# A two-layer decoder trunk with a product-key expert mixer: the table of gates built in device memory by GpSimd's accumulating transfers instead of by one-hot products on TensorE

## The chip, the cores and the metric

The kernel runs on one core of one Trainium2 chip. The metric is the device time of one execution in microseconds (us), the median of several runs. Five engines run side by side: TensorE (PE in the profile, with its weight loads apart as PEld), VectorE (DVE), ScalarE (ACT), GpSimd (POOL) and SyncE (SP), which here only issues transfers. Sixteen DMA engines move the data.

## The reference, cut to what matters

Two layers, 256 tokens, 1024 channels, all in float32. Each layer has a small token mixer (a gated convolution, then a pooling mixer) and then the part that takes most of the time, a retrieval over 16384 experts:

```python
def peer_ffn(h, w_q, k1, k2, u_tab, v_tab):        # T = 256 tokens, 8 heads, top 16, 128 keys a side
    q = (ht @ w_q).reshape(T, PEER_HEADS, 2, D_HALF)
    s1 = jnp.einsum('thd,nd->thn', q[:, :, 0], k1)
    s2 = jnp.einsum('thd,nd->thn', q[:, :, 1], k2)
    v1, i1 = lax.top_k(s1, PEER_TOPK)
    v2, i2 = lax.top_k(s2, PEER_TOPK)
    cand = (v1[..., :, None] + v2[..., None, :]).reshape(T, PEER_HEADS, PEER_TOPK * PEER_TOPK)
    sc, flat = lax.top_k(cand, PEER_TOPK)
    e1 = jnp.take_along_axis(i1, flat // PEER_TOPK, axis=-1)
    e2 = jnp.take_along_axis(i2, flat % PEER_TOPK, axis=-1)
    idx = e1 * N_KEYS + e2
    gate = jax.nn.softmax(sc.astype(jnp.float32), axis=-1)
    ...
    act = jax.nn.gelu(jnp.einsum('td,thkd->thk', xc, u_tab[ic]), approximate=False)
    out = jnp.einsum('thk,thkd->td', gc * act, v_tab[ic])
```

## The kernel before

Nothing is gathered: since 256 tokens times 128 picks touch most experts, each layer multiplies every token with all 16384 rows of `u_tab` and of `v_tab`, 128 rows to a tile. A layer runs through stages: the mixer's products, 16 "query" tiles, 128 "up" tiles, 128 "down" tiles. Every up tile gives a 128 x 256 block of expert activations (128 experts by 256 tokens), which ACT passes through Gelu into the buffer `acts`. The activations are then multiplied by a table of gates (softmax weight of expert e for token t, zero nearly everywhere), and the down tiles multiply the result with the 128 rows of `v_tab`.

Each weight tile (512 KB) takes the same road. SP loads it into one of four slots of `raw` (`load`, which waits on `low_ready` for the slot to be free); ACT rounds it to fp32r in `high` (`ahead`, `round_tile`); DVE computes the rest `low = raw - high` (`slot`, `rest_of`); PE makes three products for one (high x high, low x high, high x low). ACT and DVE work three tiles ahead (`AHEAD`). An up tile is 24 products of 256 columns, a down tile 12 of 512 columns. The order of all work is written out by hand, engine by engine, and engines meet at semaphores that count.

The picks are found on DVE beside the first 76 up tiles (`retrieval`): one pass of its loop per pair of score rows, with a `beside()` (one more tile's `low`) between the steps, nine to a pass; `numbers` turns a pass's picks into expert numbers a pass later. A softmax over all picks is made once at the end: ACT's Exp waits for `soft_in` before up tile 74, with a load of the Exp table and another of the Gelu table. Then PE transposes numbers and gates (L1289), and the table of gates is built in PSUM (`gp`) as a product of one-hot matrices: for 8 tokens at a time (a set) DVE compares the numbers with an iota (`hots`: `hot1` holds three bf16 parts of the gate at the row of e1, `hot2` a one at that of e2), PE multiplies them (`scatter`, L1267, 24 products of 64 columns a set), and DVE multiplies the activations by the result (`weigh`, L893). Half the table is built beside up tiles 80 to 127, two sets after every third tile; the other half beside the first 64 down tiles, two sets after every fourth. The last 64 down tiles of layer 0 share their time with the next layer's modulation sums (w_mod loads and L591 on DVE).

GpSimd clears a few constants at the start and is idle for the rest.

Of the kernel before, what the change touches and what calls it, by code (L numbers as in the profile page):

```python
# [5 lines left out]
F32 = mybir.dt.float32  # L6
# [7 lines left out]
P = 128  # L14
# [17 lines left out]
SETS = HALF // 2  # L32
SET = T // SETS
PAIRS = SET // 2
TURN = 76
FIRST_SET = 80
PARTS = 3
# [48 lines left out]
def program(nc, small, x_in, k_t, w_mod, conv_in, conv_out, query, up, down, pool_in, pool_group, pool_out,  # L86
# [8 lines left out]
    with ExitStack() as ctx:  # L95
# [22 lines left out]
        idx1 = sb("idx1", [P, T], BF16)  # L118
        idx2 = sb("idx2", [P, T], BF16)
        gate = sb("gate", [P, T // 2, PARTS, 2], BF16)  # L120
        hot1 = sb("hot1", [P, 2, PAIRS, PARTS, HALF, 2], BF16)
        hot2 = sb("hot2", [P, 2, PAIRS, P, 2], BF16)


        gate_rest = hot2[:].rearrange("p a b c d -> p (a b c d)").bitcast(F32)[:, 0:T]
# [44 lines left out]
        GT = part(o + 1600, T)  # L170
        SUM = part(o + 1856, ROWS)
        RS = part(o + 1872, ROWS)
        twice = hot2[:, 0, 0]
# [41 lines left out]
        pick_done, turned, turned_out = sem("pick_done"), sem("turned"), sem("turned_out")  # L215
        hot1_ready = sem("hot1_ready")
        scattered, weighted = sem("scattered"), sem("weighted")
# [26 lines left out]
        def _(sp):  # L244
# [55 lines left out]

            for layer in range(LAYERS):
# [15 lines left out]
                run(layer, "up", KEYS)  # L317
# [38 lines left out]
        @block.gpsimd  # L356
        def _(pool):
            nc.gpsimd.memset(ones[:], 1.0).then_inc(const_ready, 1)
            nc.gpsimd.memset(eps[:], EPS).then_inc(const_ready, 1)
            nc.gpsimd.memset(zeros[:], 0.0).then_inc(const_ready, 1)  # L360
            nc.gpsimd.memset(macc[:, 2:MODS].rearrange("p m n -> p (m n)"), 0.0).then_inc(const_ready, 1)

        @block.scalar
        def _(act):
# [88 lines left out]
            for layer in range(LAYERS):  # L453
# [44 lines left out]
                gelus(8, (TURN - RING - 8) // RING)  # L498
                for s in range(RING):
                    if s == 2:  # L500
                        act.wait_ge(soft_in, layer + 1)
                        nc.scalar.activation(SC, SC, ACT.Exp).then_inc(soft_exp, 1)
                        load_table(ACT.Gelu)
                    gelu(0, TURN - RING, s)


                gelus(TURN, 2 * HEADS // RING)
                act.wait_ge(turned, layer + 1)
                gelus(TURN + 2 * HEADS, (KEYS - TURN - 2 * HEADS) // RING)
# [8 lines left out]
                for half in range(2):  # L518
                    first = half * HALF

                    act.wait_ge(weighted, (2 * layer + half + 1) * SETS)
                    for s in range(AHEAD):
                        act.wait_ge(product, n0 + first + s + 1 + (RING - 1 - s if half == 0 else 0))
                        weight(first + s, s)
                    with act.Fori(0, HALF // RING - 1) as i:
                        for s in range(RING):
                            ahead(i, n0 + first, s)
                            weight(i * RING + (first + s + AHEAD), (s + AHEAD) % RING)
                    last = n0 + first + HALF - RING
                    if half == 1:  # L530
                        load_table(ACT.Sqrt)
                    ahead(0, last, 0)
                    weight(first + HALF - 1, RING - 1)
                    if half == 0:
                        for s in range(1, RING):
                            ahead(0, last, s)
# [24 lines left out]
        def _(dve):  # L561
# [20 lines left out]
            link(nc.vector.tensor_tensor(cact[:], ctmp[:], sm[:, C_C:C_C + DC], ALU.mult))  # L582
            link(nc.vector.tensor_copy(twice, sm[:, C_IOTA:C_IOTA + KEYS].unsqueeze(2).broadcast_to([P, KEYS, 2])))
# [855 lines left out]
```

## Time and profile before

| | |
|---|---|
| median of 3 runs | 1902.19 us (1902.03 to 1902.82) |
| the profiled execution, its own time | 1903.38 us |
| span of its trace | 1901.6 us |
| PE busy | 1860.2 us, 98% of the span |
| DVE busy | 1524.4 us, 80% |
| ACT busy | 858.2 us, 45% |
| POOL busy | 4.0 us |
| moved by the DMA engines | 370.46 MB, 195 GB/s on average |

The table is one execution, taken by the hardware profiler. A share of busy time is an average over all stages; the rows further down are taken stage by stage. Up tiles run in this trace from about 200 to 600 us in layer 0 and from about 1112 to 1512 us in layer 1, down tiles from 601 to 963 us and from 1514 to 1876 us.

### The profile page before, as it was taken

How to read it: one execution, taken by the hardware profiler on the slowest of the kernel's cores; microseconds unless marked ns; L12 is line 12 of the kernel's file. 1: busy time of each engine (PE TensorE's matmuls, PEld its weight loads, DVE VectorE, ACT ScalarE, POOL GpSimd, SP SyncE). 2: the span in 40 equal slices, each digit the busy share in tenths (PEclk: the TensorE clock that was granted, in tenths of full speed). 3: DMA queues.
4: the chain of work that ended last, by engine and by line, in shares of the span. 5: the costliest groups of instructions: out<-in, count | busy, mean ns of one | idle time of the engine just before them, and what ended most of it. 6: DMA issues, size and time to landing. Idle time of an engine off the chain costs nothing.

```text
span 1901.6 us, 39850 instructions
## 1 busy us (share of the span) xinstructions
PE 1860.2 (98%) x14863; PEld 1726.2 (91%) x14863; DVE 1524.4 (80%) x2634; ACT 858.2 (45%) x1281; POOL 4.0 (0%) x8
## 2 busy tenths in 40 slices
PE   5999999999999999999999999999999999999998
PEld 5999999999999888888889999999999988888887
DVE  7986689888888888888868768889788888885555
ACT  3335444454434444455444544444434444445453
POOL 0000000000000000000000000000000000000000
PEclk9999999999999999999988999999999999999999
DMA  7976455555444555688834745555544455555552
GB/s 301 335 277 236 154 179 185 177 176 170 153 166 139 171 176 167 235 325 319 321 127 168 262 158 177 179 185 185 168 146 165 138 172 165 176 187 190 197 189 99
DMA packets 101344, 370.46 MB, mean 195 GB/s; under 512 B 11168, under 2 KB 11552, under 8 KB 100640
## 3 DMA queue, kind: packets, MB, share of 16 engines
q1 hardware_dynamic: 100848, 367.43, 55.5%
q10 hardware_dynamic: 432, 2.23, 0.3%
q8 instruction: 34, 0.56, 0.1%
q14 instruction: 30, 0.25, 0.0%
HBM read 366.47 MB, written 3.15 MB: 194 GB/s over the span
## 4 chain that ended last, share of the span: by engine, by line
PE 91%; DVE 5%; DMA 2%; issue 1%; ACT 1%; SPq 0%; DVEq 0%; ACTq 0%
PE ps L1156 46%; PE acc L1315 36%; PE gp L1267 5%; DVE acts L591 2%; DVE low L572 2%; PE ps L1135 1%; PE gp L1077 1%; DMA raw<-conv_in 1%; PE gp L1256 1%; DMA acts<-w_mod 1%; PE gp L1099 0%; ACT high L371 0%; DMA raw<-conv_out 0%; PE acc L1094 0%; DVE acts L952 0%
## 5 line engine op out<-in xcount | busy, mean ns | idle before, releaser
L572 DVE TENSOR_TENSOR low<-raw,high 128x1024 fp32r<-128x1024 f32 x596 | 727.7, 1222 | 320.6 <-ACT high L371 318.5
L371 ACT ACTIVATE high<-raw 128x1024 fp32r<-128x1024 f32 x593 | 626.7, 1057 | 483.0 <-PE acc L1315 383.3
L1156 PE MATMUL ps<-mov_h,high 128*128 128x256 f32 x2656 | 761.2, 287 | 9.9 <-DVE mov_l L680 5.4
L1156 PE MATMUL ps<-mov_l,high 128*128 128x256 f32 x2656 | 755.4, 284 | 0.0
L1156 PE MATMUL ps<-mov_h,low 128*128 128x256 f32 x2656 | 755.2, 284 | 0.0
L1156 PEld LDWEIGHTS ps<-mov_h,high 128*128 128x128 f32 x2656 | 513.4, 193 | 11.5 <-issue 8.2
L1156 PEld LDWEIGHTS ps<-mov_l,high 128*128 128x128 f32 x2656 | 513.7, 193 | 0.0
L1156 PEld LDWEIGHTS ps<-mov_h,low 128*128 128x128 f32 x2656 | 513.6, 193 | 0.0
L1315 PE MATMUL acc<-high,mov_h 128*128 128x512 f32 x1024 | 402.6, 393 | 1.0 <-DVE mov_l L1009 0.8
L1315 PE MATMUL acc<-high,mov_l 128*128 128x512 f32 x1024 | 399.0, 390 | 0.0
L1315 PE MATMUL acc<-low,mov_h 128*128 128x512 f32 x1024 | 398.6, 389 | 0.0
L483 ACT ACTIVATE acts<-ps 128x256 f32 (+1 forms) x256 | 98.5, 385 | 432.2 <-PE ps L1156 432.2
L1315 PEld LDWEIGHTS acc<-high,mov_h 128*128 128x128 f32 x1024 | 192.2, 188 | 41.1 <-DVE mov_l L1009 2.2
L1315 PEld LDWEIGHTS acc<-high,mov_l 128*128 128x128 f32 x1024 | 192.2, 188 | 40.6
L1315 PEld LDWEIGHTS acc<-low,mov_h 128*128 128x128 f32 x1024 | 192.4, 188 | 38.9
L881 DVE TENSOR_TENSOR hot<-hot,gate 128x1536 bf16<-128x1536 bf16 x128 | 121.9, 952 | 0.0
L591 DVE SCALAR_TENSOR_TENSOR acts<-acts,cact 128x1024 f32<-128x1024 f32 x86 | 110.1, 1280 | 5.1 <-DMA acts<-w_mod 4.7
L1009 DVE TENSOR_TENSOR mov_l<-acts,mov_h 128x256 fp32r<-128x256 f32 x256 | 106.5, 419 | 2.7 <-ACT mov_h L515 2.7
L1267 PEld LDWEIGHTS gp<-hot 128*128 128x128 bf16 x3072 | 96.4, 97 | 9.7 <-issue 8.4
L1267 PE MATMUL gp<-hot 128*128 128x64 bf16 x3072 | 104.1, 193 | 0.0
L515 ACT ACTIVATE mov_h<-acts 128x256 fp32r (+1 forms) x256 | 101.5, 399 | 0.0
L877 DVE TENSOR_TENSOR hot<-sm,idx 128x1024 bf16<-128x1024 bf16 x128 | 87.7, 685 | 0.0
(116 smaller groups left out, 802.4 us busy)
## 6 DMA issues: line engine op xcount, KB each, us to landing
raw<-up SPq DMA_DIRECT2D x256, 512.0 KB, 3.2
raw<-down SPq DMA_DIRECT2D x256, 512.0 KB, 4.0
acts<-w_mod SPq DMA_DIRECT2D x84, 512.0 KB, 5.8
raw<-query SPq DMA_DIRECT2D x32, 512.0 KB, 3.9
raw<-conv_in SPq DMA_DIRECT2D x24, 512.0 KB, 6.8
acts<-w_mod SPq DMA_DIRECT2D x6, 1024.0 KB, 14.7
raw<-conv_out SPq DMA_DIRECT2D x8, 512.0 KB, 7.0
raw<-pool_in SPq DMA_DIRECT2D x8, 512.0 KB, 3.9
```

The costliest lines, as they stand in the source:

```text
L371: nc.scalar.activation(flat(high[s]), tile_row(s), ACT.Copy).then_inc(high_ready, 1)
L483: nc.scalar.activation(A[:, bass.ds(i * (RING * T) + (first + s) * T, T)], ps[:, s % 2, 0:T], ACT.Gelu).then_inc(evac_act, 1)
L515: nc.scalar.activation(mov_h[:, s], A[:, bass.ds(g * T, T)] if not isinstance(g, int) else A[:, g * T:(g + 1) * T], ACT.Copy).then_inc(wh_ ...
L572: nc.vector.tensor_tensor(flat(low[n % RING]), tile_row(n % RING), flat(high[n % RING]).bitcast(F32), ALU.subtract).then_inc(low_ready, 1)
L591: return nc.vector.scalar_tensor_tensor(macc[:, m], tile, c, macc[:, m], ALU.mult, ALU.add)
L877: nc.vector.tensor_tensor(hot2[:, u], number(0, P), over(idx2, P), ALU.is_equal)
L881: nc.vector.tensor_tensor(hot1[:, u].rearrange("p h n e two -> p (h n) e two"), eq.unsqueeze(2).broadcast_to([P, PAIRS, PARTS, HALF, 2]).r ...
L1009: nc.vector.tensor_tensor(mov_l[:, s], A[:, g * T:(g + 1) * T], mov_h[:, s].bitcast(F32), ALU.subtract).then_inc(wl_ready, 1)
L1077: ins = nc.tensor.matmul(gp[:, 1, m * DC + c:m * DC + c + 1], macc[:, m, c * P:(c + 1) * P], ones[:, 0:1], start=True, stop=True)
L1156: ins = nc.tensor.matmul(dst, w[s][:, c], m[:, mv], start=(first and n == 0), stop=(last and n == 2), skip_group_check=skip)
L1267: ins = nc.tensor.matmul(gp[:, u, j * HALF:(j + 1) * HALF], hot2[:, u, j // 2, :, j % 2], hot1[:, u, j // 2, n, :, j % 2], start=(n == 0), ...
L1315: ins = nc.tensor.matmul(acc[:, b, :], w[:, s, tok], flat(v[s])[:, cols], start=False, stop=(closing and n == 2), skip_group_check=True)
```

## The change

The table of gates is no longer a product on PE. It lies in device memory, one table of 16.8 MB a layer, [128 partitions e2] x [128 e1] x [256 tokens] in float32.

SP clears it with 32 transfers of 512 KB a layer from a buffer of zeros: those of layer 0 behind every second query tile (8) and each of the first 24 up tiles, those of layer 1 behind every second one of the next 64 up tiles of layer 0. The retrieval is put in order of heads: a pass of its loop now covers both halves of the tokens for one head, has its own softmax (an Exp on ACT before up tiles 11, 20, ... 74, each with its two table loads), and ends with the addresses in `dest` and the gates in `gates`. For each head GpSimd issues 32 indirect transfers (2 halves of the tokens x 16 picks), each of which adds 128 single floats, one from each partition, to the table at 128 addresses; before a half's 16 transfers it waits for all of the same half's earlier ones to have landed. When all 256 of a layer have landed, GpSimd fetches the table back in 64 pieces of 256 KB (two tiles of experts each) through a ring of four buffers `wt`, and DVE multiplies the activations by each piece (`weigh`, one piece beside each of the first 62 down tiles). The one-hot products, the transposes and the sets are gone.

```diff
+            def clear(layer, at):
+                cols = bass.ds(at, CHUNK) if not isinstance(at, int) else slice(at, at + CHUNK)
+                sp.dma_start(rows[layer][:, cols].rearrange("p (r n) -> p r n", n=2 * T),
+                             nothing[:].unsqueeze(1).broadcast_to([P, CHUNK // (2 * T), 2 * T])).then_inc(zeroed[layer], 16)
...
+                if layer == 0:
+                    for j in range(24):
+                        load(0, "up", j, j % RING)
+                        clear(0, (8 + j) * CHUNK)
+                    with sp.Fori(0, CHUNKS // 2) as i:
+                        for s in range(RING):
+                            load(0, "up", i * RING + (24 + s), s)
+                            if s % 2:
+                                clear(1, i * (2 * CHUNK) + s // 2 * CHUNK)
...
+            def add_gates(layer, p, tc):
+                if layer or p:
+                    pool.wait_ge(landed[tc], 16 * TOPK * (layer * HEADS + p))
+                for k in range(TOPK):
+                    col = (TC * p + tc) * TOPK + k
+                    nc.gpsimd.indirect_dma_start(
+                        table[layer], bass.IndirectOffsetOnAxis(ap=DEST[:, col:col + 1], axis=0),
+                        GT[:, col:col + 1], None, compute_op=ALU.add).then_inc(landed[tc], 16)
+            def fetch(layer, i, s, free):
+                if free is not None:
+                    pool.wait_ge(weighted, free)
+                at = i * (WRING * 2 * T) + s * 2 * T
+                cols = bass.ds(at, 2 * T) if not isinstance(at, int) else slice(at, at + 2 * T)
+                nc.gpsimd.dma_start(wt[:, s], rows[layer][:, cols]).then_inc(wt_in[s], 16)
+            for layer in range(LAYERS):
+                pool.wait_ge(zeroed[layer], 16 * CHUNKS)
+                for p in range(HEADS):
+                    pool.wait_ge(picked, layer * HEADS + p + 1)
+                    for tc in range(TC):
+                        add_gates(layer, p, tc)
+                for tc in range(TC):
+                    pool.wait_ge(landed[tc], 16 * TOPK * HEADS * (layer + 1))
+                for s in range(WRING):
+                    fetch(layer, 0, s, layer * WPAIRS - WRING + s + 1 if layer else None)
...
-                gelus(8, (TURN - RING - 8) // RING)
-                for s in range(RING):
-                    if s == 2:
-                        act.wait_ge(soft_in, layer + 1)
-                        nc.scalar.activation(SC, SC, ACT.Exp).then_inc(soft_exp, 1)
+                exps = {(HEADS + 1) * p + 11: p for p in range(HEADS)}
+                for j in range(8, SCRATCH):
+                    if j in exps:
+                        p = exps[j]
+                        act.wait_ge(soft_in, HEADS * layer + p + 1)
+                        sc = SC[:, TC * p * TOPK:TC * (p + 1) * TOPK]
+                        nc.scalar.activation(sc, sc, ACT.Exp).then_inc(soft_exp, 1)
                         load_table(ACT.Gelu)
...
+            def weigh(layer, j):
+                dve.wait_ge(wt_in[j % WRING], 16 * (layer * (WPAIRS // WRING) + j // WRING + 1))
+                a = A[:, 2 * j * T:2 * (j + 1) * T]
+                nc.vector.tensor_tensor(a, a, wt[:, j % WRING], ALU.mult).then_inc(weighted, 1)
...
                 dve.wait_ge(evac_act, 2 + layer * (16 + KEYS) + 16 + HALF)
-                k = 0
-                for j in range(FIRST_SET, KEYS):
-                    slot(n0 + j)
-                    if (j - FIRST_SET) % 3 == 2:
-                        two_sets(0, k)
-                        k += 2
+                weigh(layer, 0)
+                weigh(layer, 1)
...
                 for j in range(HALF):
                     slot(n0 + j)
-                    if j + AHEAD < HALF:
-                        low_weight(j + AHEAD)
-                    if j % 4 == 2:
-                        two_sets(1, j // 4 * 2)
+                    if j + 2 < WPAIRS:
+                        weigh(layer, j + 2)
+                    low_weight(j + AHEAD)
...
-                        up_tile(i, FIRST_SET, s, 12)
-                        if s % 3 == 1:
-                            scatter(0, i, s // 3 * 2, 8)
-                            scatter(0, i, s // 3 * 2 + 1, 8)
```

On PE, at the end of the second tile of four in the first half of the down stage, these rows stand before (L1315 are a down tile's products, L1267 those of two sets, 24 each; the others are loop registers):

```order
1451 L1315 MATMUL acc<-low,mov_h 128x512
1452 L1315 MATMUL acc<-high,mov_l 128x512
1453 L1264 ISA
1454 L1267 MATMUL gp<-hot 128x64 x24
1455 L1264 REGISTER_ALU
1456 L1267 MATMUL gp<-hot 128x64 x24
1457 L1322 REGISTER_ALU
1458 L1323 REGISTER_ALU
1459 L1315 MATMUL acc<-high,mov_h 128x512
```

and now (L1299 are a down tile's products):

```order
913 L1299 MATMUL acc<-low,mov_h 128x512
914 L1299 MATMUL acc<-high,mov_l 128x512
915 L1306 REGISTER_ALU
916 L1307 REGISTER_ALU
917 L1299 MATMUL acc<-high,mov_h 128x512
```

One tile's products now follow the last one's with nothing between; the same holds at the up tiles from 80 on.

On DVE, in the retrieval's second pass, behind the last search for candidates (L827 before) and at the next tile's `low` (L572), these rows stand before:

```order
211 L821 MAX acts<-acts 128x8 x2
212 L769 TENSOR_REDUCE acts<-acts 128x2x32
213 L572 TENSOR_TENSOR low<-raw,high 128x1024
214 L827 MAX_INDEX acts<-acts 128x8 x2
215 L572 TENSOR_TENSOR low<-raw,high 128x1024 x2
```

and now (L906 is that search, L627 that `low`; `gates` and `dest` are what GpSimd's transfers read):

```order
218 L900 MAX acts<-acts 128x8 x2
219 L831 RECIPROCAL acts<-acts 128x2
220 L833 TENSOR_REDUCE acts<-acts 128x2x32
221 L627 TENSOR_TENSOR low<-raw,high 128x1024
222 L906 MAX_INDEX acts<-acts 128x8 x2
223 L911 TENSOR_TENSOR acts<-acts 128x32
224 L840 SCALAR_TENSOR_TENSOR acts<-acts 128x32
225 L842 TENSOR_TENSOR gates<-acts 128x32
226 L846 SCALAR_TENSOR_TENSOR dest<-acts,tok 128x32
227 L627 TENSOR_TENSOR low<-raw,high 128x1024 x2
```

A pass has gained short instructions of its own softmax and addresses (five of them here, two more earlier in the pass), and the first head's addresses are there only at the end of the second pass.

On POOL, before, the last instructions are the clearing of constants:

```order
8 L360 MEMSET zeros 128x128
9 L361 MEMSET acts 128x4096
10 L95 UNCONDITIONAL_BRANCH
```

and now, for layer 0 (with what the instruction waits for; the rows of heads 1 to 6 read like those of head 7, which are the last three ahead of the fetches):

```order
10 L387 MEMSET nothing 128x512
11 L396 DMA table<-gates,dest 4194304x1 [waits picked,zeroed0]
12 L396 DMA table<-gates,dest 4194304x1 x31
13 L396 DMA table<-gates,dest 4194304x1 [waits landed0,picked]
...
38 L396 DMA table<-gates,dest 4194304x1 x15
39 L396 DMA table<-gates,dest 4194304x1 [waits landed1]
40 L396 DMA table<-gates,dest 4194304x1 x15
41 L406 DMA wt<-table 128x512 [waits landed1,landed0]
42 L406 DMA wt<-table 128x512 x3
```

POOL's queue now holds 256 indirect transfers a layer, and no fetch can leave before the last of them has landed.

## Rows read from the trace of the kernel before

**Rows 1.** The page: busy time, and the chain that ended last, by line.

```profile
PE 1860.2 (98%) x14863; PEld 1726.2 (91%) x14863; DVE 1524.4 (80%) x2634; ACT 858.2 (45%) x1281; POOL 4.0 (0%) x8
...
PE ps L1156 46%; PE acc L1315 36%; PE gp L1267 5%; DVE acts L591 2%; DVE low L572 2%; PE ps L1135 1%; PE gp L1077 1%; DMA raw<-conv_in 1%; PE gp L1256 1%; DMA acts<-w_mod 1%; PE gp L1099 0%; ACT high L371 0%; DMA raw<-conv_out 0%; PE acc L1094 0%; DVE acts L952 0%
```

**Rows 2.** The chain in order of time: start us, length us, what.

```profile
229.19 201.59 PE ps L1156 x1680
430.78 0.66 PE gp L1289 x6
444.40 8.71 PE ps L1156 x72
454.58 8.71 PE ps L1156 x72
608.51 11.01 PE acc L1315 x48
621.00 11.01 PE acc L1315 x48
801.37 160.77 PE acc L1315 x708
1141.75 201.59 PE ps L1156 x1680
```

**Rows 3.** The same chain where the up stage ends and the down stage begins.

```profile
597.04 2.96 PE ps L1156 x24
...
601.31 5.74 PE acc L1315 x24
```

**Rows 4.** Stretches: length, busy time (x) of PE, PEld, DVE, ACT, POOL, PEclk, DMA share, GB/s.

```profile
229.00:430.00 201.00, 201.00 (x1677) 201.00 (x1676) 174.48 (x467) 98.31 (x144) 0.00 (x0) 1.00 0.51 180
608.00:793.00 185.00, 185.00 (x1405) 153.84 (x1402) 162.20 (x241) 80.78 (x119) 0.00 (x0) 1.00 0.52 170
802.00:962.00 160.00, 160.00 (x708) 132.47 (x707) 132.30 (x155) 79.97 (x118) 0.00 (x0) 1.00 0.87 320
```

**Rows 5.** DVE's groups, 225 to 400 us: shapes, count, busy us, mean ns, idle before.

```profile
L572 DVE TENSOR_TENSOR low<-raw,high 128x1024 fp32r<-128x1024 f32 x60 | 73.1, 1218 | 22.9 <-ACT high L371 22.9
L754 DVE TENSOR_TENSOR acts<-acts,sm 128x1024 f32<-128x1024 uint32 x7 | 8.5, 1208 | 0.0
```

**Rows 6.** Groups over the whole run.

```profile
L1009 DVE TENSOR_TENSOR mov_l<-acts,mov_h 128x256 fp32r<-128x256 f32 x256 | 106.5, 419 | 2.7 <-ACT mov_h L515 2.7
L893 DVE TENSOR_TENSOR acts<-acts,gp 128x512 f32<-128x512 f32 x128 | 81.8, 681 | 0.0
```

**Rows 7.** DVE in order of time: the second pass's end, and a short instruction.

```profile
255.70 0.42 DVE L827 FIND_INDEX8 acts<-acts 128x8 uint32<-128x256 f32 x1
256.61 1.23 DVE L572 TENSOR_TENSOR low<-raw,high 128x1024 fp32r<-128x1024 f32 x1 [0.48 <-ACT high L371]
413.33 0.17 DVE L749 TENSOR_SCALAR acts<-acts 128x32 uint32<-128x32 uint32 x1
```

**Rows 8.** ACT in order of time around the Exp of layer 0.

```profile
419.70 1.28 ACT L502 ACT_TABLE_LOAD   x1
421.43 1.28 ACT L386 ACT_TABLE_LOAD   x1
423.92 0.37 ACT L483 ACTIVATE acts<-ps 128x256 f32<-128x256 f32 x1
```

**Rows 9.** One issue on SP's queue (start, length), then transfers' median us to landing.

```profile
850.44 0.33 SPq L256 DMA_DIRECT2D raw<-down  x1
...
out<-acts SPq DMA_DIRECT2D x4, 256.0 KB, 2.1
acts<-k_t ACTq DMA_DIRECT2D x1, 128.0 KB, 3.1
```

**Rows 10.** DMA, first 12 us: GB/s by slice, then queues (packets, MB, share).

```profile
GB/s 0 0 0 0 0 0 71 81 104 355 438 413 409 355 314 328 396 423 410 410 451 396 300 382 437 437 437 410 369 396 355 396 423 410 355 437 410 410 437 410
q10 hardware_dynamic: 144, 0.13, 5.7%
```

More of the change, by code:

```diff
@@ L117, in program @@
         zeros = sb("zeros", [P, P], BF16)
[L118 to L125, printed above, removed]
+        GT = sb("gates", [P, T], F32)
+        DEST = sb("dest", [P, T], U32)
+        tok = sb("tok", [P, TC], F32)
+        wt = sb("wt", [P, WRING, 2 * T], F32)
+        nothing = sb("nothing", [P, 2 * T], F32)
+        table = [nc.dram_tensor(f"table{n}", (P * KEYS * T, 1), F32, kind="Internal").ap() for n in range(LAYERS)]
+        rows = [v.rearrange("(p n) one -> p (n one)", p=P) for v in table]
         iota = sm[:, C_IOTA:C_IOTA + KEYS].bitcast(BF16).rearrange("p (n two) -> p n two", two=2)
@@ L214, in program @@
         soft_in, soft_exp = sem("soft_in"), sem("soft_exp")
[L215 to L217 removed]
+        picked, pick_done = sem("picked"), sem("pick_done")
+        zeroed = [sem(f"zeroed{n}") for n in range(LAYERS)]
+        landed = [sem(f"landed{n}") for n in range(TC)]
+        wt_in = [sem(f"wt_in{n}") for n in range(WRING)]
+        weighted = sem("weighted")
         wh_ready, wl_ready = sem("wh_ready"), sem("wl_ready")
@@ L361, in _ @@
             nc.gpsimd.memset(macc[:, 2:MODS].rearrange("p m n -> p (m n)"), 0.0).then_inc(const_ready, 1)
+            nc.gpsimd.memset(nothing[:], 0.0).then_inc(const_ready, 1)
+            def add_gates(layer, p, tc):
[22 more added lines that the diff above has]
+                    fetch(layer, 0, s, layer * WPAIRS - WRING + s + 1 if layer else None)
+                with pool.Fori(0, WPAIRS // WRING - 1) as i:
+                    for s in range(WRING):
+                        fetch(layer, i + 1, s, i * WRING + (layer * WPAIRS + s + 1))
         @block.scalar
@@ L516, in weight @@
                                          else A[:, g * T:(g + 1) * T], ACT.Copy).then_inc(wh_ready, 1)
[L518 to L536, printed above, removed]
+                for s in range(AHEAD):
+                    act.wait_ge(product, n0 + RING)
+                    act.wait_ge(weighted, layer * WPAIRS + s // 2 + 1)
+                    weight(s, s)
+                with act.Fori(0, KEYS // RING - 1) as i:
+                    for s in range(RING):
+                        ahead(i, n0, s)
+                        act.wait_ge(weighted, i * (RING // 2) + (layer * WPAIRS + (s + AHEAD) // 2 + 1))
+                        weight(i * RING + (s + AHEAD), (s + AHEAD) % RING)
+                last = n0 + KEYS - RING
+                load_table(ACT.Sqrt)
+                ahead(0, last, 0)
+                weight(KEYS - 1, RING - 1)
                 def evac(b):
@@ new lines, in down_banks @@
+                def down_banks(s, banks, closing):
+                    for b in banks:
+                        tok = slice(b % 2 * P, (b % 2 + 1) * P)
+                        cols = slice(b // 2 * 512, (b // 2 + 1) * 512)
+                        for n, (v, w) in enumerate(((high, mov_h), (low, mov_h), (high, mov_l))):
+                            ins = nc.tensor.matmul(acc[:, b, :], w[:, s, tok], flat(v[s])[:, cols], start=False,
+                                                   stop=(closing and n == 2), skip_group_check=True)
+                        if closing and b < 3:
+                            ins.then_inc(acc_done, 1)
+                    return ins
```

238 lines of the change are left out of this document (86 added, 152 removed).

## The prediction

> **What bounds the kernel now.** I read the page first. PE is busy for 98% of the span, and the chain that ended last is PE for nine tenths: 46% up tiles (L1156), 36% down tiles (L1315), 5% one-hot products (L1267) [rows 1]. So the share that the change removes lies on the path itself. Then I read the chain in order of time for prices without overlap. The steady up stage is one piece, 1680 products in 201.59 us: 0.120 us each, 2.880 us a tile. The steady down stage is 708 products in 160.77 us: 0.2271 us each, 2.725 us a tile [rows 2]. The stretches show what the other engines have left there: DVE is busy 87% beside the retrieval, 88% in the first half of the down stage, 83% in the second; the DMA engines 51%, 52% and 87% [rows 4].
>
> **What is removed.** In the up stage three tiles with two sets take 454.58 - 444.40 = 10.18 us, three plain tiles 8.64: two sets cost 1.54 us, 16 times a layer, 24.6 us. In the down stage four tiles with two sets take 621.00 - 608.51 = 12.49 us, four plain ones 10.90: 1.59 us, 16 times, 25.4 us. The transposes are 0.66 us [rows 2]. Per layer 50.7 us, together 101.4 us, all of it on PE's path.
>
> **What is added on PE: nothing.** The rest counts only where something becomes late.
>
> DVE, retrieval. A pass gains seven short instructions. The nearest row, 32 elements, is 0.17 us [rows 7]; with waits for their predecessors between them I take up to 0.25, so 1.2 to 1.75 us a pass. DVE's idle time there is 22.9 us in 60 tiles, 3.4 us per pass of nine tiles, and all of it is waiting for ACT's `high` [rows 5]. That covers it: nothing. Without the cover, each further us a pass costs 16 us in all.
>
> ACT, softmax. Exp and two table loads hold ACT from 419.70 to 422.71 and the Gelu of tile 74 ends at 423.92 + 0.37 = 424.29 [rows 8]. Tile 76 needs it at 229.19 + 68 x 2.880 = 425.03 [rows 2], and the 201.59 us piece ran through that place without a gap. This now happens eight times a layer, never more often than every nine tiles: nothing, with 0.74 us to spare. `soft_in` leaves DVE before the `low` of that tile's successor, so ACT finds it there.
>
> DVE, down stage. A tile needs low 1.22, mov_l 0.42 and the product with a fetched piece; the nearest row is L893, 128x512, 0.68 [rows 5, 6]. 2.32 us against 2.725: nothing.
>
> Clears. In the query stage and beside the first 24 up tiles 1.049 MB have to move per 2.88 us, 364 GB/s. With reads alone the engines gave 355 to 451 in most slices after the start [rows 10], and 320 at a share of 0.87, which would be 368 at full share [rows 4]. Writes of this kind aren't in the trace. Between nothing and, at 320 GB/s, 40 tiles x 0.40 = 16 us; I take 3, since the demand meets the full-share rate and a load has four slots to land in. SP's queue gains one issue of 0.33 us per tile [rows 9]: nothing. The fetches bring the down stage to 192 + 96 = 288 GB/s, less than the 320 beside which PE ran without a gap: nothing.
>
> **The queue that decides: POOL.** It issues 256 indirect transfers a layer, and the first down tile stands behind the last. When can it begin? The first head's addresses follow the second pass's last search, which ends at 256.12, by about 1 us: 257 [rows 7]. The last clear of layer 0 goes out at about the same time and takes some 4 us more: 261. Layer 1 is the same, 912.56 us later [rows 2], without the clear. When must it end? Tile 8 starts at 229.19, so up tiles now end at 229.19 + 120 x 2.880 = 574.8; before, the first down product came 1.31 us behind the last up tile [rows 3], so 576.1. Ahead of it stand: landing 2.1 and the fetch 2.1 (the quickest kind in the trace), its issue 0.33 [rows 9], the product 0.68, mov_h and mov_l 0.9: about 6.1, so the last transfer must leave by 570. That is 309 us in layer 0 and 313 in layer 1, **1.21 us per transfer**. Each 0.1 us more costs 256 x 2 x 0.1 = 51 us, and the gain is gone at 1.21 + 98/512 = 1.41 us. Heads come every nine tiles (25.9 us), so below 0.81 us POOL waits for DVE and it doesn't matter.
>
> The trace has no transfer from POOL, so its pitch has to be bounded. From below the nearest row is an issue on SP's hardware queue, 0.33 us; from above a transfer waited out each time, 3.1 us for 128 KB from issue to landing [rows 9]. POOL writes 128 descriptors by program and reads 128 addresses, but doesn't wait for landings within a head (16 transfers to a semaphore, two semaphores by turns). I take about 1 us, the geometric middle of the two ends. Then 256 us fit into 309, and the cost is nothing.
>
> The Trainium skill, DMA: Bandwidth & Descriptors, Latency and other measured facts, gives about 1 us to the first byte from GpSimd; were that the pitch, the queue would be hidden, with 0.2 us a transfer to spare. The same page, Anatomy of one DMA, fits about 2.0 us fixed per transfer; were they not overlapped, it would be 512 x 0.79 = 404 us of stall. No row of this case tells which.
>
> **The sum.** 1903.4 (the profiled execution's own time, 1.2 above the median of the runs) - 101.4 + 3 = **1805 us**.
>
> **Rivals.**
>
> *POOL's own pitch is over 1.41 us: slower.* One mechanism: at the end of each up stage PE stands until the last head has landed. For it: software descriptors, two sides, one address read for every float. Against it: three issues of SP would fit into the allowance. At 1.8 us: 1805 + 512 x 0.59 = 2107; at 2.07: 2245.
>
> *POOL is late by less than it gains (1.21 to 1.41):* 1810 to 1900.
>
> *DVE holds POOL off.* Of the 175 us of the retrieval's stretch L572 and L754, which read two operands from SBUF for 1.2 us each, take 81.6, 47% [rows 5]. Should POOL's read of addresses have to wait for such an instruction's end, that is 0.47 x 0.6 = 0.28 us per transfer, and POOL's own pitch may only be 0.93. With an own pitch of 1.2 it would give 1805 + 512 x 0.27 = 1943, slower. The trace can't show it, since POOL is idle. The Trainium skill, SBUF — State Buffer, Who interferes with whom, says just this of DVE instructions with two SBUF inputs beside a GpSimd instruction that reads SBUF; it infers that descriptor writing isn't touched.
>
> *The DMA engines can't take the small adds.* The 144 packets of the ACT queue in the first 12 us, 0.9 KB each, took 5.7% of 16 engines: 76 ns each [rows 10]. 128 adds are 128 reads and 128 writes, 16 packets an engine, 1.2 us per transfer. 256 of them and the weight stream's 51% [rows 4] need 312 + 176 = 488 us of 346: 142 us late a layer, 1805 + 284 = 2089. Against it: packets in flight overlap, so 76 ns may be mostly waiting.
>
> **How the numbers follow.** I know POOL's pitch only between 0.33 and 3.1 us, so I spread it evenly over the ratio: 58% lies below 1.21, 65% below 1.41, 82% below 2.07. The lock would put the first two at 46% and 55% or so, and the engines' load takes some more. So: hidden 0.46; late but less than the gain 0.08; within 0.2% (about what a measurement of this kernel can tell from no change) 0.02; own pitch over 1.41 0.29; lock 0.07; engines 0.08. Faster 0.54, same 0.02, slower 0.44. The range goes from 1797 (no cost for the clears, and 5 us for gaps at the stages' joints that may shrink) to 2245, beyond which 0.18 remain. Cases of both signs hold much; the hidden case's own range is 1797 to 1825.
>
> **What the new profile would show.** L1267 gone from the chain, and 120 up tiles from the ninth on as one piece of 346 us (right); a gap of PE between the last up product and the first down product of more than 2 us, with POOL behind it (wrong: then the distance from one indirect transfer to the next beside it is the pitch, and which of the three it is shows in the DMA share and in whether it is shorter where DVE runs no two-operand work). DVE's idle time in the retrieval still behind `high`; if PE waits for `low` there, a pass has become too long. PE waiting for `high` behind DMA in the first 24 up tiles would be the clears.

## The result, and the profile after

The changed kernel takes 2233.87 us (median of four executions, 2233.14 to 2235.66) against 1902.49 us before: a ratio of 1.174 (95% interval 1.172 to 1.176). I had predicted 1805. The time lies in the stated range, on the side of the rivals: not faster by 5%, but slower by 17%.

The page of the changed kernel, busy time and the costliest group of POOL, answers to [rows 1]:

```profile
PE 1760.5 (79%) x11779; PEld 1635.3 (73%) x11779; DVE 1305.8 (58%) x2341; ACT 895.7 (40%) x1337; POOL 960.8 (43%) x649
...
PEclk9999999999655589999999999999985557999999
...
L396 POOL DMA_INDIRECT table<-gates,dest x512 | 887.2, 1733 | 801.9 <-DVE dest L846 385.3
```

PE's work shrank from 1860.2 to 1760.5 us, as it should. But its share of the span fell from 98% to 79%, and in two places its clock line drops to 5: there PE does nothing. The waits name the place (engine, line, what was waited for: us in all, times, longest):

```profile
PE acc L1299 <- DVE mov_l L1028: 432.0, 2, 218.7
DVE acts L929 <- DMA wt<-table: 430.6, 3, 217.5
```

Twice, once a layer, the first down product waits 213 to 219 us for its moving operand `mov_l`, which waits for the first fetched piece of the table. The longest wait of DVE has almost the same length, so nothing lies between but the chain that the prediction had listed. What the fetch waited for stands in POOL's order of time (start, length, instruction, idle time before it), layer 0, first the beginning and then the end of the table:

```profile
265.90 1.78 POOL L396 DMA_INDIRECT table<-gates,dest  x1 [260.74 <-DMA table<-nothing]
267.98 1.56 POOL L396 DMA_INDIRECT table<-gates,dest  x1 [0.30 <-issue]
...
785.80 1.55 POOL L396 DMA_INDIRECT table<-gates,dest  x1 [0.30 <-issue]
789.41 2.25 POOL L406 DMA_DIRECT2D wt<-table  x4 [2.06 <-DMA table<-gates,dest]
```

The 256 transfers of layer 0 begin at 265.90 and end at 787.35, 521 us, where 309 were free. And stretches (length, busy time and count of PE, PEld, DVE, ACT, POOL, clock, DMA share, GB/s) show where they were when PE ran out of up tiles, with [rows 4] as their counterpart:

```profile
229.00:575.00 346.00, 346.00 (x2887) 345.96 (x2886) 240.24 (x567) 184.94 (x273) 265.71 (x142) 1.00 0.86 247
576.00:788.00 212.00, 0.00 (x0) 0.00 (x0) 0.00 (x0) 0.00 (x0) 176.63 (x115) 0.51 0.22 3
```

Up to 575 us PE works without a gap; POOL has got through 142 of 256. Then only POOL works, 115 transfers in 212 us (one counts on both sides), 1.85 us each: 1.55 busy and 0.30 of "issue" before the next. So the reader can see the whole of the excess in one row: four engines at zero.

### The profile page after: what moved, and what is told of

Same layout as the page of the kernel before. It is cut to its first block and busy times, and to the rows that moved or that the text cites. A ratio compares the mean times of both kernels' runs of the same rounds, so it can differ in the third digit from the quotient of the medians.

```text
span 2233.7 us, 34220 instructions
## 1 busy us (share of the span) xinstructions
PE 1760.5 (79%) x11779; PEld 1635.3 (73%) x11779; DVE 1305.8 (58%) x2341; ACT 895.7 (40%) x1337; POOL 960.8 (43%) x649
## 5 line engine op out<-in xcount | busy, mean ns | idle before, releaser
L396 POOL DMA_INDIRECT table<-gates,dest x512 | 887.2, 1733 | 801.9 <-DVE dest L846 385.3
L627 DVE TENSOR_TENSOR low<-raw,high 128x1024 fp32r<-128x1024 f32 x596 | 727.5, 1223 | 444.4 <-ACT high L430 443.7
L1299 PE MATMUL acc<-high,mov_h 128*128 128x512 f32 x1024 | 400.5, 391 | 432.0 <-DVE mov_l L1028 432.0
L1299 PEld LDWEIGHTS acc<-high,mov_h 128*128 128x128 f32 x1024 | 193.1, 189 | 472.2 <-DVE mov_l L1028 432.3
L1299 PE MATMUL acc<-low,mov_h 128*128 128x512 f32 x1024 | 399.8, 390 | 0.0
L1299 PE MATMUL acc<-high,mov_l 128*128 128x512 f32 x1024 | 399.6, 390 | 0.0
L929 DVE TENSOR_TENSOR acts<-acts,wt 128x512 f32<-128x512 f32 x128 | 87.5, 684 | 430.6 <-DMA wt<-table 430.6
L542 ACT ACTIVATE acts<-ps 128x256 f32<-128x256 f32 (+1 forms) x256 | 98.1, 383 | 343.5 <-PE ps L1170 343.3
L1299 PEld LDWEIGHTS acc<-high,mov_l 128*128 128x128 f32 x1024 | 193.0, 189 | 40.7
L1299 PEld LDWEIGHTS acc<-low,mov_h 128*128 128x128 f32 x1024 | 193.1, 189 | 39.9
L406 POOL DMA_DIRECT2D wt<-table x128 | 69.1, 541 | 267.5 <-DVE acts L929 263.1
L1091 PEld LDWEIGHTS gp<-ones,acts 128*128 128x128 f32 x192 | 25.7, 215 | 11.3 <-DVEq L658 9.8
```

Source lines behind the costliest of these rows:

```text
L396: nc.gpsimd.indirect_dma_start(table[layer], bass.IndirectOffsetOnAxis(ap=DEST[:, col:col + 1], axis=0), GT[:, col:col + 1], None, compute ...
L406: nc.gpsimd.dma_start(wt[:, s], rows[layer][:, cols]).then_inc(wt_in[s], 16)
L542: nc.scalar.activation(A[:, bass.ds(i * (RING * T) + (first + s) * T, T)], ps[:, s % 2, 0:T], ACT.Gelu).then_inc(evac_act, 1)
L627: nc.vector.tensor_tensor(flat(low[n % RING]), tile_row(n % RING), flat(high[n % RING]).bitcast(F32), ALU.subtract).then_inc(low_ready, 1)
L929: nc.vector.tensor_tensor(a, a, wt[:, j % WRING], ALU.mult).then_inc(weighted, 1)
L1091: ins = nc.tensor.matmul(gp[:, 1, m * DC + c:m * DC + c + 1], macc[:, m, c * P:(c + 1) * P], ones[:, 0:1], start=True, stop=True)
```

## The experiments

Each series ran the kernel before beside it: 1900.73 us beside e1, e3, e4 and e5, 1901.80 beside e2, e6 and e7, 1901.62 beside e8 and e9. So times of different series compare to about 2 us. e3, e4, e5, e7 and e8 are one execution each.

**e1: 8 of the 16 picks of each head** (128 transfers a layer; the gates of the other picks are left out).

```diff
+PICKS = 8
...
-                for k in range(TOPK):
+                for k in range(PICKS):
```

> The changed kernel with only the first 8 of each head's 16 picks added to the table (128 transfers a layer instead of 256; the other half of the gates is left out). Theory Q, the queue's length: POOL leaves about one transfer per 2.04 us from 266 us on, so the last leaves at about 266 + 261 = 527 us, before the up stage ends at 575; both waits of PE for the first down tile vanish and the time is 1805 us (1798 to 1812). Rival R, something else that the change adds costs too (clears, eight Exps a layer, a busier DVE, the fetches): the two waits vanish but the time stays clearly above, 1820 to 1900. Rival D, the transfers' landing and the DMA engines and not POOL's issuing set the end: the wait shrinks by less than the 128 transfers' 238 us a layer would allow, and a wait of tens of us stays.

1800.61 us (four executions, 1798.36 to 1802.58), ratio 0.947 (0.945 to 0.948). In the chain in order of time (start, length) the joint has closed up: 119 up tiles are one piece, and 123 down tiles the next:

```profile
231.09 342.73 PE ps L1171 x2856
578.14 334.86 PE acc L1300 x1476
```

With the queue hidden, the kernel is where the prediction's sum puts it. Rival D, the landing of the transfers, is out too: PE waits 1.1 us in both layers together. So the removal is worth what was read from [rows 2], and clears, fetches, the longer passes and the eight Exps cost nothing that can be seen. What failed is POOL's queue alone.

**e2: 12 of 16 picks** (192 a layer, the rest left out), the same edit with 12.

> Only 12 of the 16 picks of each head are added to the table (192 transfers a layer instead of 256; the gates of the last four picks are left out of the computation). Theory F (the whole excess is the POOL queue: 1.55 us a transfer and 0.30 between two, longer while VectorE is busy): about 144 of the 192 are out when the up products end at 575 us, the other 48 take 1.85 us each, 89 us, and then the fetch and the first weighting, some 8 us; so the down products start some 97 us late in each layer, less what the changed kernel's own start needs there, and the kernel takes 1805 + 2 x 96, about 1997 us. Rival C (the cost of the table is not the number of transfers before the deadline, but sets in with the last ones, for instance because the additions to one place queue up): the time lies in proportion between that of 8 picks, 1801, and that of 16, 2234, which gives 2017, or stays near 2234.

1998.38 us (two executions), ratio 1.051 (1.049 to 1.053). The expectation by theory F was 1997; PE waits 99.7 us a time at most:

```profile
PE acc L1300 <- DVE mov_l L1029: 195.9, 2, 99.7
```

The time isn't in proportion to the transfers: 128 cost nothing, the next 64 a layer 198 us in all, the next 64 another 235. It is a queue with a deadline, some 140 transfers long. Rival C's proportion would have given 2017.

**e3: the same transfers as plain writes** (a gate that two heads share is kept once instead of summed).

```diff
-                        GT[:, col:col + 1], None, compute_op=ALU.add).then_inc(landed[tc], 16)
+                        GT[:, col:col + 1], None).then_inc(landed[tc], 16)
```

> The same 256 transfers a layer, but plain writes instead of additions (a gate that two heads share is kept once only). Theory Q: POOL's own time is that of writing 128 pairs of descriptors and reading 128 addresses, the addition is done by the DMA engines: 1.55 us busy and 1.85 us from one to the next, as before, time 2234 us within 10. Rival A, the addition costs POOL descriptors of its own (a second read of each cell): 1.2 us busy or less, and 512 x 0.35 = 180 us or more off the time, 2055 us.

**e4: 64 rows a transfer** (the gates of half of the tokens are left out).

```diff
-                        GT[:, col:col + 1], None, compute_op=ALU.add).then_inc(landed[tc], 16)
+                        GT[0:64, col:col + 1], None, compute_op=ALU.add).then_inc(landed[tc], 16)
```

> Each of the 256 transfers a layer takes the picks of 64 tokens only, partitions 0 to 63 (the gates of the other half of the tokens are left out). Theory row: POOL's 1.55 us are mostly per row: 0.8 us busy, 1.1 from one to the next, 256 of them (282 us) fit and the time is 1805 us (within 10). Rival fixed: most of the 1.55 us is paid per instruction: 1.3 us busy or more, pitch 1.6 or more, and a wait of PE of at least 100 us a layer stays, 2010 us or more.

e3 took 1942.76 us and e4 2131.33: in both the rival held and not the theory. POOL's instructions on the table (ns, least, median, most; first and last start), of the changed kernel, of e3 and of e4:

```profile
L396 POOL DMA_INDIRECT table<-gates,dest x512: 1537/1547/3237, 265.9 to 1861.2; - x171
```

```profile
L396 POOL DMA_INDIRECT table<-gates,dest x512: 954/959/3344, 264.2 to 1568.9; - x171
```

```profile
L396 POOL DMA_INDIRECT table<-gates,dest x512: 1391/1407/3347, 264.1 to 1756.5; - x171
```

The addition costs POOL itself 0.59 of its 1.55 us a transfer. Half the rows save only 0.14: by these two points, an estimate, about 2.2 ns a row stand on a fixed 1.27 us ((1547 - 1407) / 64, and 1547 less 128 of these). And even plain writes, 0.96 + 0.30 = 1.26 us apart at best, miss the allowance of 1.21; PE still waited 140.6 us in e3, which is 2% slower than the kernel before.

**e5: does DVE hold POOL off?** Extra DVE work in the stall, results unused: in layer 0 additions that take `nothing` twice, in layer 1 sums over `nothing`.

```diff
+                if layer == 0:
+                    for q in range(150):
+                        last = did(nc.vector.tensor_tensor(spare[:, q % 2 * 512:(q % 2 + 1) * 512], nothing[:], nothing[:],
+                                                           ALU.add))
...
+                else:
+                    for q in range(150):
+                        last = did(nc.vector.tensor_reduce(single[:, q % 2:q % 2 + 1], nothing[:], AX_X, ALU.add))
...
```

> The changed kernel, whole, with 150 short DVE instructions of 512 elements put into the stretch in which every other engine waits for POOL: in layer 0 additions of two operands from SBUF (0.68 us each, about 102 us), in layer 1 reductions of one operand (about 98 us). Theory L, a transfer that starts while DVE reads two operands from SBUF waits for that instruction's end: in layer 0's stretch the mean of a transfer rises from 1.55 us to 1.8 or 1.9, the wait of PE there grows by about 15 us, and in layer 1's stretch it stays at 1.55 us. Rival: any DVE work slows POOL: both rise. Rival: none does, and the longer transfers of the up stage come from the weight stream in the DMA engines: both stay at 1.55 us and the time at 2234 us.

2234.88 us, and POOL's transfers seemed to keep their length beside both kinds (mean 1572 and 1571 ns). That spoke against the rival of the lock. The means hide a difference, though: 1571 takes in one transfer of 2.56 us that had begun beside the last `low`, and beside the sums themselves all are 1.54 to 1.56. Beside the additions three are longer, the first one (1.86 us at 576.44) and these two:

```profile
645.20 1.56 POOL L397 DMA_INDIRECT table<-gates,dest  x1 [0.30 <-issue]
647.07 2.09 POOL L397 DMA_INDIRECT table<-gates,dest  x1 [0.30 <-issue]
649.47 2.09 POOL L397 DMA_INDIRECT table<-gates,dest  x1 [0.30 <-issue]
651.87 1.54 POOL L397 DMA_INDIRECT table<-gates,dest  x1 [0.30 <-issue]
```

The trace of the changed kernel itself spoke for the lock more plainly. DVE and POOL in order of time in the up stage of layer 0:

```profile
504.57 1.23 DVE L627 TENSOR_TENSOR low<-raw,high 128x1024 fp32r<-128x1024 f32 x1 [1.65 <-ACT high L430]
507.68 1.23 DVE L627 TENSOR_TENSOR low<-raw,high 128x1024 fp32r<-128x1024 f32 x1 [1.88 <-ACT high L430]
```

```profile
504.64 2.58 POOL L396 DMA_INDIRECT table<-gates,dest  x1 [0.30 <-issue]
507.52 1.55 POOL L396 DMA_INDIRECT table<-gates,dest  x1 [0.30 <-issue]
```

The first transfer begins 0.07 us into L627 and lasts 1.03 us longer than 1.55; the second is 0.16 us ahead of the next L627 and lasts 1.55. Where two-operand instructions stand one behind the other, the hold can reach over more than one: the transfer at 271.70 begins with an L627 and is held over it and over the 512 elements of L876 behind it.

```profile
271.70 1.22 DVE L627 TENSOR_TENSOR low<-raw,high 128x1024 fp32r<-128x1024 f32 x1
272.84 0.68 DVE L876 TENSOR_TENSOR acts<-acts 128x512 f32<-128x512 f32 x1
```

```profile
271.70 3.24 POOL L396 DMA_INDIRECT table<-gates,dest  x1 [0.30 <-issue]
```

So I looked for what the probe had been missing.

**e7: two different operands, and larger ones.**

```diff
+                def two(n, q, in1):
+                    return did(nc.vector.tensor_tensor(spare[:, q * n:(q + 1) * n], A[:, 0:n], in1, ALU.add))
+
+                if layer == 0:
+                    for q in range(80):
+                        last = two(512, q % 2, nothing[:])
...
+                    for q in range(40):
...
+                        last = two(1024, 0, A[:, 1024:2048])
+                        for h in range(2):
+                            last = did(nc.vector.tensor_reduce(single[:, h:h + 1], nothing[:], AX_X, ALU.add))
+                else:
+                    for q in range(60):
...
+                        last = two(1024, 0, A[:, 1024:2048])
+                    for q in range(80):
...
+                        last = two(512, q % 2, A[:, 0:512])
```

> The changed kernel, with VectorE given extra work while it waits for the table (results unused). Layer 0: 80 additions of 512 elements of two different buffers (acts and nothing), end to end, then 40 times one addition of 1024 elements of two places of acts and two sums over 512 elements of one operand. Layer 1: 60 additions of 1024 elements end to end, then 80 additions of 512 elements that take the same place of acts twice. Theory L2 (a transfer that is issued while a VectorE instruction with two different operands runs is held until that ends; the same operand twice doesn't do it): the transfers beside the first three kinds last longer, by some 0.3 us on the average beside 512 elements and 0.6 beside 1024, in the mixed part only those that begin during the addition, and those beside the last kind stay at 1.55. Rival S (size: only instructions of 1024 elements hold it): the first kind leaves 1.55, the 1024 ones lengthen it. Rival G (what holds the transfers in the up stage is not VectorE's operands but the output buffer, which PE or the DMA engines share there): all stay at 1.55 to 1.57, as with the earlier probe. The kernel's time rises by what the additions cost the queue, by 0 (rival G) to about 50 us.

2276.63 us, 43 more than without the additions. POOL beside the 512-element additions, and beside the 1024-element ones with sums between:

```profile
596.81 1.55 POOL L397 DMA_INDIRECT table<-gates,dest  x1 [0.30 <-issue]
598.66 1.54 POOL L397 DMA_INDIRECT table<-gates,dest  x1 [0.30 <-issue]
...
700.53 2.14 POOL L397 DMA_INDIRECT table<-gates,dest  x1 [0.30 <-issue]
702.98 2.15 POOL L397 DMA_INDIRECT table<-gates,dest  x1 [0.30 <-issue]
```

By the letter this was rival S, the size, and two different buffers don't matter. But DVE's own rows show a trap:

```profile
595.61 10.53 DVE L1024 TENSOR_TENSOR mov_l<-acts,nothing 128x512 fp32r<-128x512 f32 x17
```

17 additions in 10.53 us are 0.619 each, and three of them 1.858: just the distance of two transfers. In step with them, every transfer begins at a joint between two additions and has nothing to wait for. e5's additions had the same pitch (28 in 17.29 us). Once in step, such a train looks the same with a lock and without; only the transfers that fall out of step tell, as the two in e5 did. In layer 1 of e7, too, the second transfer beside the additions of 512 elements that take one place twice is held, and then they fall into step:

```profile
1755.14 2.09 POOL L397 DMA_INDIRECT table<-gates,dest  x1 [0.30 <-issue]
1757.54 1.56 POOL L397 DMA_INDIRECT table<-gates,dest  x1 [0.30 <-issue]
```

**e8: pitches that don't divide 1.85**, one place of `acts` taken twice: 1024 elements in layer 0, 736 in layer 1, 64 additions and then 64 sums.

```diff
+                for kind, n in (((two, 1024), (total_of, 1024)), ((two, 736), (total_of, 736)))[layer]:
+                    for q in range(64):
+                        last = kind(n)
...
```

> The changed kernel with extra VectorE work in the stall (results unused), one after the other: layer 0 has 64 additions of 1024 elements that take one and the same place of acts twice, then 64 sums over 1024 elements of one operand; layer 1 the same with 736 elements. In both earlier probes three instructions of 512 elements took 1.856 us (0.619 each), and a transfer with its gap takes 1.85: the transfers could begin at a boundary every time without being held, so these two probes could not show a hold. 1024 elements (about 1.22 us) and 736 (about 0.88) don't divide 1.85 so. Theory L3 (a transfer is held until the end of any VectorE instruction of two operands in whose course it is issued, whatever its size and operands; one operand doesn't do it): beside the additions the transfers follow each other at a multiple of the additions' pitch, about 2.44 us for 1024 elements and 2.6 for 736, and last longer by what is missing, 0.6 and 0.7 us; beside the sums they last 1.55. Rival S2 (a hold only from 1024 elements on): 736 leaves 1.55. Rival B (two different buffers or places are needed): all stay at 1.55. Rival O (any VectorE instruction holds them): the sums lengthen them as the additions do.

2255.93 us. DVE's pieces first, then POOL beside the additions of 1024, the sums of 1024, and the additions of 736:

```profile
575.08 80.61 DVE L1024 TENSOR_TENSOR mov_l<-acts 128x1024 fp32r<-128x1024 f32 x64 [0.27 <-PE ps L1184]
655.72 80.23 DVE L1027 TENSOR_REDUCE single<-acts 128x1 f32<-128x1024 f32 x64
1673.20 61.36 DVE L1024 TENSOR_TENSOR mov_l<-acts 128x736 fp32r<-128x736 f32 x64 [0.27 <-PE ps L1184]
```

```profile
622.13 2.21 POOL L397 DMA_INDIRECT table<-gates,dest  x1 [0.30 <-issue]
624.65 2.21 POOL L397 DMA_INDIRECT table<-gates,dest  x1 [0.30 <-issue]
...
690.75 1.55 POOL L397 DMA_INDIRECT table<-gates,dest  x1 [0.30 <-issue]
692.60 1.55 POOL L397 DMA_INDIRECT table<-gates,dest  x1 [0.30 <-issue]
...
1705.59 1.62 POOL L397 DMA_INDIRECT table<-gates,dest  x1 [0.30 <-issue]
1707.52 1.60 POOL L397 DMA_INDIRECT table<-gates,dest  x1 [0.30 <-issue]
```

The additions of 1024 come every 80.61 / 64 = 1.26 us, and the transfers every 2.52, twice that, each 0.66 us longer. The additions of 736 come every 0.959 us and the transfers every 1.92, again twice, so they are longer by only 0.06; I had expected 2.6 from a pitch of 0.88 that I had guessed too small, so that two would not have sufficed. Sums over one operand, as long as the additions, change nothing. That is theory L3: two operands from SBUF, at each of the three sizes tried (1024, 736 and 512 elements) and even if they are one place; S2, B and O are out.

The sums differ from the additions in one thing more: they write a single element. That the operands count and not what is written shows in the changed kernel. MATCH_REPLACE8 reads one operand of 256 elements and writes as many, and the transfer that is issued 0.04 us into it isn't held; it is the same in each of the six such pairs beside the retrieval of layer 0:

```profile
279.24 0.40 DVE L893 MATCH_REPLACE8 acts<-acts 128x256 f32<-128x256 f32 x1
```

```profile
279.28 1.55 POOL L396 DMA_INDIRECT table<-gates,dest  x1 [0.30 <-issue]
```

**e6 and e9: a version that divides the work.** POOL builds the table for tokens 0 to 127 alone, 128 transfers a layer. The gates of tokens 128 to 255 come from one-hot products, sets of four tokens where the kernel before had eight. It computes everything. The core of the edit:

```diff
-                    for tc in range(TC):
-                        add_gates(layer, p, tc)
+                    add_gates(layer, p, 0)
...
+                a = a[:, :, H + k * SET:H + (k + 1) * SET]
+                g = gp[:, u, 0:SET * HALF].rearrange("p (t g) -> p g t", t=SET)
+                nc.vector.tensor_tensor(a, a, g, ALU.mult).then_inc(set_done, 1)
...
-                a = A[:, 2 * j * T:2 * (j + 1) * T]
...
+                a = A[:, 2 * j * T:2 * (j + 1) * T].rearrange("p (g t) -> p g t", t=T)[:, :, 0:H]
```

> The whole computation, divided: GpSimd's transfers build the table for tokens 0 to 127 alone (128 a layer, a table half as large), and the gates of tokens 128 to 255 are made as before by one-hot products, 32 sets of four tokens for each half of the values instead of 64. Theory F: 128 transfers are out before the up products end (with 8 picks they ended at 546 us), so nothing waits; the sets left cost half of the 101.4 us that the change took away, and the clears half, so the kernel takes 1903 - 51 + 2, about 1855 us, 2.5 % less than before. Rival D (the two ways get into each other's way: VectorE's one-hot operations have two operands and hold up the transfers, the transfers' own time beside them rises over 2.4 us, and VectorE, which makes both the sets and the weights, becomes late): the table is late by up to 50 us a layer, or the sets are, and the kernel takes 1880 to 1960 us.

> The divided kernel of the half of the tokens once more, unchanged: it had one execution of 4552 us among five between 1851 and 1858 us. If that was a disturbance from outside, these six lie at 1851 to 1859 us and the ratio to the kernel before is again 0.975; if it belongs to the kernel (its transfers being slow to be served at times), a second one of that kind comes up in about every sixth.

1855.56 us (median of six executions), ratio 0.975 (0.974 to 0.976), and in the second series of the same kernel 1855.96 us (five executions), ratio 0.976 (0.975 to 0.977); I had expected 1855. One execution of the first six took 4552 us. It is in the median (1854.46 without it) and not in the ratio; none like it came up among the next five, which does not exclude one in every eleven or so, and its cause is not known. PE does 1813.8 us of work in a span of 1854.9, and POOL is in time:

```profile
L411 POOL DMA_INDIRECT table<-gates,dest x256: 1537/1565/3334, 260.7 to 1436.3; - x128
L421 POOL DMA_DIRECT2D wt<-table x128: 536/536/605, 568.4 to 1648.7; - x128
```

The up products, which the sets make longer again, end at 584.5 in layer 0. The first fetch leaves at 568.4, 16 us before that, and in layer 1 it leaves over 30 us before. A larger share of the tokens than half was not tried. A transfer lasts 1.81 us in the mean here, under the 2.4 of rival D.

This version's fetches show one thing more. They are plain transfers, issued by POOL too, and DVE's two-operand instructions don't hold them. The one below (DVE's row, then POOL's) is issued 0.50 us before the end of an L650, the `low` of this kernel, and lasts its 0.54 all the same:

```profile
602.66 1.23 DVE L650 TENSOR_TENSOR low<-raw,high 128x1024 fp32r<-128x1024 f32 x1
```

```profile
603.39 0.54 POOL L421 DMA_DIRECT2D wt<-table  x1 [3.92 <-DVE acts L1008]
```

This is the fastest version that I have that computes the whole.

## Why the prediction was wrong, step by step

- **What is removed: right.** e1, where nothing waits, is 1800.61, and the sum was 1805. Its 3 us for the clears can't be seen there: from 156 to 229 us, beside the clears, PE is busy 72.91 of 73 us in both kernels, although the DMA share rose from 0.57 to 0.91.
- **Nothing added on PE, DVE and ACT: right.** PE is without a gap from 229 to 575 us, the piece of 346 us that the prediction asked for. DVE's idle time between 225 and 400 us, all of it behind `high`, went from 22.9 us [rows 5] to 21.1.
- **When POOL begins and must end: right within 5 us.** 265.90 instead of 261; the end of the up stage at 575 as worked out. From the last transfer to the first down product, 787.35 to 794.71, it took 7.4 us instead of 6.1.
- **"I take about 1 us, the geometric middle of the two ends": this step failed.** The pitch is 1.85 us, 1.55 of work and 0.30 between two, and with what DVE adds 521 / 256 = 2.04. The allowance of 1.21 and the point of 1.41 (its own sum gives 1.40) were right, so the sign hung on this one number, of which the prediction itself said that no row gave it. The middle of two ends a factor of nine apart is no measurement: SP's 0.33 us is the price of another kind of issue altogether. Of what it leaves out e3 and e4 show the parts: 0.59 us for the addition, and of the 1.55 us about 1.27 (the estimate above) that don't depend on the rows.
- **The rivals.** POOL's own pitch over 1.41 was the right one: 1805 + 512 x (1.85 - 1.21) = 2133. DVE's lock came on top of it instead of in its place: POOL's 512 transfers took 887.2 us where 512 x 1.547 are 792.1, so 95 us in all, 0.19 a transfer (I had priced 0.28). 2133 + 95 = 2228, 6 short of the result: 5 for the later beginning in layer 0, 2.6 for the longer way from the last transfer, twice, and 2 for the clock (below), less the 4 by which 1805 lies above e1. (Layer 1 was allowed 4 us more, 313, than the 1.21 takes; so the sum closes to some 5 us.) That split is arithmetic from the rows; a kernel without the lock and otherwise the same was not run. Where it fell, POOL's busy time and count show, beside the retrieval and then beside `low` alone (length, busy, clock, DMA share, GB/s):

```profile
262.00:430.00 168.00, 139.42 (x82) 1.00 0.97 275
450.00:574.00 124.00, 107.72 (x53) 1.00 0.68 183
```

- That is 1.70 and 2.03 us a transfer, so 0.15 and 0.48 of hold. I had taken 0.28 from the share of two-operand work beside the retrieval, as if transfers began at random; what counts is where in L627's period of 2.88 us the next one begins.
- The other rivals. Late by less than the gain: wrong. The DMA engines as the bound: wrong. In the stall, with a transfer every 1.85 us, their share is 0.22, so 0.41 us a transfer instead of 1.2. Both factors were too high: the software queue's 16426 packets there, in 115 transfers, are 143 each and not 256, and 45 ns each and not 76. In the up stage, too, a transfer that starts clear of DVE's two-operand work takes 1.55 us, even at the DMA share of 0.97. Whether quicker transfers would have met the clears and the weights there (e3's plain writes, lighter on the engines, left the share at 0.85) was not run.
- **The clock** was not in the sum. In the stall it stands at 0.51, the 1.2 GHz level, after PE had been idle, and the first products back run at it (they start 0.43 us apart up to 797.87 and 0.23 apart from 798.30 on):

```profile
794.71 0.80 PE L1299 MATMUL acc<-high,mov_h 128*128 128x512 f32 x1 [218.72 <-DVE mov_l L1028]
```

- From e1 to the changed kernel the time grows by 433.3 us and PE's wait by 430.9, so this and all else is worth some 2 us.

## What to carry to other kernels

Work that is moved onto an idle engine has a deadline: work out the pitch that it allows (here 309 us / 256 = 1.21) and, before building on it, measure the one price that the trace lacks; twenty transfers in an otherwise empty kernel would have decided this case. When the queue turns out too slow by less than a factor of two, give it the part that it can do in time and leave the rest where it was: half of the tokens gave back half of the gain. A probe for contention must not run at a pitch that divides the period of what it is to disturb; e5 and e7 did, and e5's means alone would have acquitted the lock; where a probe's means agree, look at its rows one by one.

## What the runs showed of the hardware

- An indirect accumulating transfer of 128 single floats occupies GpSimd for 1.55 us, with 0.30 us between two of them; without the addition 0.96 (e3); with 64 rows 1.41 (e4). Plain transfers of 128 rows (`wt<-table`) took 0.54.
- Such a transfer that is issued while a DVE instruction with two operands in SBUF runs is held until about 0.12 us before that ends (2.58 instead of 1.55 us beside L627), and sometimes over the next such instruction as well (3.24 us). One that began earlier isn't disturbed, one-operand instructions don't hold it, and GpSimd's plain transfers aren't held (0.54 us with and without, e6). The Trainium skill, SBUF — State Buffer, Who interferes with whom, says that a two-input DVE instruction contends with a GpSimd instruction that reads SBUF, and the runs agree, with 0.66 us more a transfer in e8. It also infers that such an instruction leaves descriptor generation alone. The plain transfers agree with that; for transfers that take their addresses from SBUF the measurement differs. That it is the reading of addresses that is held fits both, but no run here took it apart from the rest of such a transfer.
- The two figures of the Trainium skill that the prediction had weighed, about 1 us to the first byte and 2.0 us fixed for a transfer (DMA: Bandwidth & Descriptors), lie on either side of the pitch of 1.85 us, and neither is it.
